# Conformer convolution of a two-block transformer: VectorE's first taps in PSUM banks of their own, and an earlier norm

## What is computed

```python
def conformer_conv(h, w_in, b_in, dw, dw_b, ln_g, ln_b, w_out, b_out):
    D = h.shape[-1]
    u = h @ w_in + b_in                       # 1024 -> 2048
    u = u[..., :D] * jax.nn.sigmoid(u[..., D:])
    u = causal_dwconv(u, dw) + dw_b           # 31 taps for each channel
    u = jax.nn.silu(layernorm(u, ln_g, ln_b))
    return u @ w_out + b_out                  # 1024 -> 1024, added to x
```

## Time and profile before

| what | value |
|---|---|
| median of 3 runs | 2368.12 us |
| the profiled execution | 2368.39 us |
| its span, first to last instruction | 2366.7 us |
| mean granted TensorE clock over the span | 0.989 |
| inputs, memory and conv_out's first two tiles in the profile | about 1636 to 1842 us |

### The profile page before, as it was taken

How to read it: one execution, slowest core, us unless ns; L and a number is a source line. 1 busy time by engine, 2 the same in 40 slices (tenths; PEclk the granted TensorE clock), 3 DMA queues, 4 the chain that set the end, 5 groups by cost and what they waited for, 6 DMA issues and landing times.

```text
span 2366.7 us, 34912 instructions
## 1 busy us (share of the span) xinstructions
PE 2309.9 (98%) x13442; PEld 1853.8 (78%) x13442; DVE 1109.2 (47%) x1870; ACT 977.0 (41%) x1655; POOL 1105.6 (47%) x952
## 2 busy tenths in 40 slices
PE   8999999999999999989999999999999999999998
PEld 6777578888867777868878888888786878888887
DVE  3445553113143887554334651652697333561562
ACT  5556652222256563444333231235665433322232
POOL 3443444544532342337525454456775625445344
PEclk9999999999999999999999999999999999999999
DMA  4211013222411220024212333222223312233232
GB/s 153 98 63 52 19 63 97 94 96 97 156 63 54 63 63 20 4 90 143 91 52 89 98 107 98 89 97 81 72 72 125 98 45 89 89 104 110 81 97 71
DMA packets 58475, 197.71 MB, mean 84 GB/s; under 512 B 6752, under 2 KB 11616, under 8 KB 57824
## 3 DMA queue, kind: packets, MB, share of 16 engines
q1 hardware_dynamic: 54000, 189.85, 24.8%
q10 hardware_dynamic: 4336, 5.96, 0.8%
HBM read 193.69 MB, written 2.10 MB: 83 GB/s over the span
## 4 chain that ended last, share of the span: by engine, by line
PE 52%; DVE 2%; POOL 1%; ACT 1%; issue 0%; DVEq 0%; POOLq 0%; ACTq 0%
PE ps L408 12%; PE ps L409 12%; PE ps L410 12%; PE ps L520 3%; PE ps L519 3%; PE ps L521 3%; PE ps L3240 1%; PE ps L3263 1%; DVE ps L3457 1%; PE ps L494 1%; PE ps L496 1%; PE ps L495 0%; POOL conv_y L3414 0%; PE ps L3470 0%; POOL w_lo L544 0%
## 5 line engine op out<-in xcount | busy, mean ns | idle before, releaser
L543 POOL TENSOR_TENSOR w_lo<-raw,w_hi 128x512 fp32r<-128x512 f32 x342 | 447.5, 1308 | 900.6 <-ACT w_hi L535 900.4
L408 PE MATMUL ps<-ahead_hi,w_hi 128*128 128x512 f32 x1216 | 478.2, 393 | 0.3 <-DVE ahead_lo L810 0.3
L410 PE MATMUL ps<-ahead_hi,w_lo 128*128 128x512 f32 x1216 | 473.3, 389 | 0.0
L409 PE MATMUL ps<-ahead_lo,w_hi 128*128 128x512 f32 x1216 | 473.2, 389 | 0.0
L544 POOL TENSOR_TENSOR w_lo<-raw,w_hi 128x512 fp32r<-128x512 f32 x342 | 451.1, 1319 | 0.0
L535 ACT ACTIVATE w_hi<-raw 128x1024 fp32r<-128x1024 f32 x342 | 353.2, 1050 | 181.2 <-PE ps L521 90.3
L823 DVE TENSOR_TENSOR x_stream<-x_stream,ps 128x512 f32<-128x512 f32 x79 | 54.3, 688 | 455.7 <-PE ps L410 270.9
L408 PEld LDWEIGHTS ps<-ahead_hi,w_hi 128*128 128x128 f32 x1216 | 228.3, 188 | 50.4 <-issue 2.4
L409 PEld LDWEIGHTS ps<-ahead_lo,w_hi 128*128 128x128 f32 x1216 | 228.3, 188 | 49.3 <-issue 2.4
L410 PEld LDWEIGHTS ps<-ahead_hi,w_lo 128*128 128x128 f32 x1216 | 228.2, 188 | 47.7
L3603 ACT ACTIVATE ffn_s<-ps 128x512 f32<-128x512 f32 x44 | 26.4, 599 | 322.2 <-DVE ps L3631 322.2
(11 more groups left out here) (499 smaller groups left out, 4536.0 us busy)
## 6 DMA issues: line engine op xcount, KB each, us to landing
raw<-in_wall SPq DMA_DIRECT2D x346, 512.0 KB, 3.6
...
lora_a<-in_lora_a ACTq DMA_DIRECT2D x1, 1280.0 KB, 11.3
...
```

Source lines behind the costliest of these rows:

```text
L408: pe.matmul(out, hi, src.hi[:, t, 0:width], start=first, stop=False)
L409: pe.matmul(out, hi, src.lo[:, t, 0:width], start=False, stop=False)
L410: return pe.matmul(out, lo, src.hi[:, t, 0:width], start=False, stop=last)
L543: e.tensor_tensor(self.w.lo[:, s, 0:512], self.raw[:, s, 0:512], as_float(self.w.hi[:, s, 0:512]), ALU.subtract)
```

## The change

- **First two tiles in their own banks.** VectorE's 19 taps of channel tiles 0 and 1 are gathered in PSUM banks 2 and 3, which are free until TensorE's taps of tiles 2 and 3, instead of on top of TensorE's seven. The first tap is a multiply with the bias added. So they need only `conv_u` and begin right behind its first tile: 16 steps of tile 0 alone, then steps of both in turn, then tile 1 alone. Each tile ends with two additions into `conv_y` (own bank, then TensorE's bank) where there was one. A step on one tile alone waits for the step just before it. The two tiles are 42 steps (OWN_OPS), and the pairs of tiles 2 and 3, 4 and 5, 6 and 7 now begin at steps 42, 82 and 122.
- **The table** of steps is (0, 16, 32, 42, 60, 78, 98, 116, 134). The list that says where TensorE does its taps is not changed.
- **New waits.** TensorE's taps of tile 2 and 3 wait until the own banks are added to `conv_y`.
- **Five mean sums.** GpSimd adds `conv_y` of tiles 0 to 3 together (three additions, behind channel tiles 4, 6 and 7), and TensorE sums that and tiles 4 to 7: five matmuls for eight.
- **The norm sooner.** Mean sums stand behind memory tiles 7 and 10 (6, 7 and 11 before), variance sums behind 11 and 12 (13 and 14), ScalarE's squares and root two steps earlier, and silu and rounding of tiles 0 to 2 one step earlier, the other five in the last step ahead of the copy of the values.
- **Next tiles paired.** conv_out makes tiles 0 and 1 together: for each tile of `ys` first the three matmuls of tile 0, then those of tile 1.

The diff, cut to its core:

```diff
@@ Linear.tensor, for the first four tiles of a stage
+            if first_group and self.paired:
+                self.two_tiles(pe, sums)
+            for j in range(2 if first_group and self.paired else 0, 4):
...
+    def two_tiles(self, pe, sums):
+        used, lo_r = self.marks[0], self.marks[3]
+        for q in range(self.kt):
+            pe.wait_ge(self.ready.sem, self.ready(q + 1))
+            for j in range(2):
+                if q == 0:
+                    pe.wait_ge(lo_r.sem, lo_r(j + 1))
+                mm = sums(self.k.ps[:, self.bank + j, 0:self.width], j, q, 0, q == 0, q == self.kt - 1)
...
@@ class Conformer
-    BOUNDS = (0, 0, 10, 28, 40, 58, 80, 98, 118)
+    DVE_TAPS = TAPS - PE_TAPS - POOL_TAPS
+    OWN_OPS, ALONE = 2 * (DVE_TAPS + 2), 16
+    BOUNDS = (0, 16, 32, 42, 60, 78, 98, 116, 134)
...
@@ inputs_pool
+            if f in (4, 6, 7):
+                self.mean_pool(g, {4: 1, 6: 2, 7: 3}[f])
...
@@ inputs_vector
+        if f == 0:
+            v.wait_ge(self.padz.sem, self.padz(1))
+        v.wait_ge(self.free.sem, self.free(2 * f + 2 + RING))
         self.taps_vector(v, self.BOUNDS[f], self.BOUNDS[f + 1])
...
+    def own_place(self, m, step):
+        steps, alone = self.OWN_OPS // 2, self.ALONE
+        if m == 0:
+            return step if step < alone else alone + 2 * (step - alone)
+        return alone + 2 * step + 1 if step < steps - alone else steps + step
...
+    def own_step(self, v, m, step):
+        k, own, y = self.k, self.k.ps[:, 2 + m, :], self.y[:, m, :]
+        t = PE_TAPS + POOL_TAPS + step
+        if step:
+            v.wait_ge(self.added.sem, self.added(self.own_added(m, step - 1)))
+        if step == 0:
+            v.tensor_scalar(own, self.u[:, m, t:t + T], self.tap(m, t), k.vec("cdw_b", m), ALU.mult, ALU.add
+                            ).then_inc(self.added.sem, 1)
+        elif step < self.DVE_TAPS:
+            v.scalar_tensor_tensor(own, self.u[:, m, t:t + T], self.tap(m, t), own, ALU.mult, ALU.add
+                                   ).then_inc(self.added.sem, 1)
+        elif step == self.DVE_TAPS:
+            v.wait_ge(self.pooled.sem, self.pooled((POOL_TAPS - 1) * (m + 1)))
+            v.tensor_tensor(y, y, own, ALU.add).then_inc(self.added.sem, 1)
+        else:
+            v.wait_ge(self.summed.sem, self.summed(m + 1))
+            v.tensor_tensor(y, y, k.ps[:, m, :], ALU.add).then_inc(self.kept.sem, 1)
...
@@ taps_vector
-        for pair, n in (divmod(at, self.PAIR_OPS) for at in range(first, last)):
-            base = pair * (self.PAIR_OPS - 2)
+        for at in range(first, min(last, self.OWN_OPS)):
+            for m in range(2):
+                for step in range(self.DVE_TAPS + 2):
+                    if self.own_place(m, step) == at:
+                        self.own_step(v, m, step)
+        for pair, n in (divmod(at - self.OWN_OPS, self.PAIR_OPS) for at in range(max(first, self.OWN_OPS), last)):
+            pair += 1
...
@@ taps_tensor
             pe.wait_ge(self.kept.sem, self.kept(m - 3))
+        elif m >= 2:
+            pe.wait_ge(self.added.sem, self.added(self.own_added(m - 2, self.DVE_TAPS)))
@@ mean_tensor, and the new mean_pool
+        if m == 3:
+            pe.wait_ge(self.pooled_y.sem, self.pooled_y(3))
...
-        mm = pe.matmul(self.k.ps[:, 0, :], self.k.ones[:, :], self.y[:, m, :], start=(m == 0), stop=(m == KD - 1))
+        mm = pe.matmul(self.k.ps[:, 0, :], self.k.ones[:, :], self.rt[:, :] if m == 3 else self.y[:, m, :],
+                       start=(m == 3), stop=(m == KD - 1))
...
+    def mean_pool(self, g, m):
+        g.wait_ge(self.kept.sem, self.kept(m + 1))
...
+        g.tensor_tensor(self.rt[:, :], self.y[:, 0, :] if m == 1 else self.rt[:, :], self.y[:, m, :], ALU.add
+                        ).then_inc(self.pooled_y.sem, 1)
@@ memory_tensor
-        for m in {6: (0, 1, 2), 7: (3, 4, 5), 11: (6, 7)}.get(t, ()):
+        for m in {7: (3, 4, 5), 10: (6, 7)}.get(t, ()):
             self.mean_tensor(pe, m)
-        for m in {13: (0, 1, 2, 3), 14: (4, 5, 6, 7)}.get(t, ()):
+        for m in {11: (0, 1, 2), 12: (3, 4, 5, 6, 7)}.get(t, ()):
             self.variance_tensor(pe, m)
@@ memory_scalar
+        if m == 2 * KD - 1:
+            self.fed_scalar(act, 3, KD)
         self.keys.taken(act, 4, m)
-        if m == 12:
+        if m == 10:
...
-        if m == 14:
+        if m == 12:
...
-        if m == 15:
...
+        if m == 14:
+            self.fed_scalar(act, 0, 3)
@@ conv_ffn stages, the projection conv_out
-                       fill=again.kept)
+                       fill=again.kept, paired=True)
```

More of the change, by code:

```diff
@@ L343, in __init__ @@
     def __init__(self, k, m_tiles, kt, src, act=None, vector=None, pool=None, width=T, feed=None, unroll=False,
-                 norm=False, bank=0, ready=None, prev=None, fill=None, release=False, middle=None, packed=False, held=0, early=0, norm_at=0, between=None, tokens=None):
+                 norm=False, bank=0, ready=None, prev=None, fill=None, release=False, middle=None, packed=False, held=0, early=0, norm_at=0, between=None, tokens=None, paired=False):
+        self.paired = paired
         self.tokens = tokens
@@ L477, in tensor @@
                               ).then_inc(summed.sem, 1)
+    def two_tiles(self, pe, sums):
[6 more added lines that the diff above has]
+                mm = sums(self.k.ps[:, self.bank + j, 0:self.width], j, q, 0, q == 0, q == self.kt - 1)
+                if q == self.kt - 1:
+                    mm.then_inc(used.sem, 1)
+        if self.fill is not None:
+            for j in range(2):
+                self.fill(pe, j)
     def token_chunk(self, pe, m):
@@ new lines, in own_added @@
+    def own_added(self, m, step):
+        at, last = self.own_place(m, step), self.DVE_TAPS + 1
+        return at + 1 - sum(1 for n in range(2) if self.own_place(n, last) < at)
+    def own_step(self, v, m, step):
[15 more added lines that the diff above has]
+            v.tensor_tensor(y, y, k.ps[:, m, :], ALU.add).then_inc(self.kept.sem, 1)
@@ L3572, in memory_scalar, with fed_scalar @@
                 act.activation(self.sq[:, n, :], y[:, n, :], ACT.Square).then_inc(sq.sem, 1)
[L3573 removed]
+        if m == 12:
             act.wait_ge(va.sem, va(1))
             act.activation(self.rt[:, :], k.ps[:, 1, :], ACT.Sqrt, scale=1.0 / D, bias=k.bias[1e-5]).then_inc(rt.sem, 1)
[L3576 to L3581 removed]
+        if m == 14:
+            self.fed_scalar(act, 0, 3)
+    def fed_scalar(self, act, first, last):
+        n1, n2, hi = self.norm[6:9]
+        for n in range(first, last):
+            act.wait_ge(n1.sem, n1(n + 1))
+            act.activation(self.y[:, n, :], self.y[:, n, :], ACT.Silu, bias=self.k.vec("cln_b", n)).then_inc(n2.sem, 1)
+            act.wait_ge(n2.sem, n2(n + 1))
+            act.activation(self.out.hi[:, n, :], self.y[:, n, :], ACT.Copy).then_inc(hi.sem, 1)
 def conv_ffn(k, layer, at, tmp, ready, gain=None, closing=False):
```

19 lines of the change are left out of this document (9 added, 10 removed).

## The result

The changed kernel takes 2376.21 us (median of 15 runs) beside 2367.86 us for the kernel before on the same chip: 8.35 us more. The ratio on record is 1.004, 95% interval 1.0033 to 1.0047, so 7.8 to 11.1 us slower. 2378.3 us was forecast, with slower as the likeliest case. One of the 15 runs was disturbed (7291 us) and is left out of the ratio. The profiled execution took 2377.03 us, its span 2375.3 us, mean clock 0.988 (2368.39, 2366.7 and 0.989 before).

What follows compares the result with a forecast made beforehand. TensorE, busy 98% of the span, was taken as the bound. 14.4 (A and B) + 1.8 - 2.6 - 3.4 = +10.2 us on the profiled 2368.39 us, or 2378.3 us against the median; range 2372.0 to 2382.5 us.

Steps and rivals of the forecast that it cites:

- A: Before tile 4's taps: VectorE waits for tile 3's taps, holding the next scalings, so TensorE idles; +8.3 us.
- B: Before tile 6's taps: VectorE waits for tile 5's taps, holding the next scalings, so TensorE idles; +6.8 us.
- C: Memory stage: GpSimd's third mean addition delays a weight chunk for which TensorE waits; +1.8 us.
- D: Mean sums: five instead of eight save TensorE three matmuls; -2.6 us.
- E: Norm to conv_out: 9.0 us lost before goes, a late second chunk costs 3.4 idle and 2.2 slow clock; -3.4 us.
- First inputs: nothing: First channel tiles: early single steps delay tile 1's taps by 0.1 to 0.3 us, about as much returning at tile 2.
- held scalings cost nothing: Rival on tiles 4 and 6: VectorE catches up before TensorE needs their taps; 14.4 us less, 2364 us; chance 0.06.
- only the first wait bites: Rival on tile 6: VectorE meets tile 5's taps without holding tile 6; 6.8 us less, 2371.5 us; chance 0.06.
- VectorE's end: nothing: Mean sums: VectorE ends later, 1807.6 instead of 1800.4, but TensorE needs it only at about 1813; no cost.
- it would be there in time: Rival at conv_out: silu does not hold the second chunk; 3.4 and 2.2 us go, 2372.7 us; chance 0.04.
- the price of slow clock: Slow matmuls behind four TensorE gaps, priced 2.9, 2.6, 0.8 and 2.2 us: 8.5 us of the additions, the least certain.
- 1.55 us for each gap: Lower clock price for the four TensorE gaps: 6.2 us of slow clock in all, giving 2376.0 us.

Runs made afterwards that it cites:

- e5: e4 without the own banks, VectorE's taps and their table as in the kernel before: 2357.19 us, 0.9956 to 0.9979 of the kernel before.
- e4: Changed kernel with both e2's table and e3's later silu and rounding: 2359.73 us, 0.9966 to 0.9985 of the kernel before.
- e1: Changed kernel with steps needing tile 5's taps moved behind the product of tile 6: 2369.93 us, 1.0005 to 1.0022 of the kernel before.
- e2: Changed kernel with e1's move, and steps needing tile 3's taps behind tile 4's product: 2364.16 us, 0.9982 to 1.0001 of the kernel before.
- e9: Changed kernel with eight mean sums on TensorE and no additions on GpSimd: 2374.56 us, 1.0021 to 1.0041 of the kernel before.
- e7: e4 with earlier low part, VectorE on the two oldest ready tiles, third mean addition in the memory stage: 2354.05 us, 0.9942 to 0.997 of the kernel before.
- e3: Changed kernel with all silu and rounding behind the split of conv_out's second chunk: 2370.36 us, 1.0007 to 1.0025 of the kernel before.
- e8: Kernel before with only the pairing of conv_out's first two tiles: 2362.72 us, 0.9985 to 1.0003 of the kernel before.

## Why the prediction was right, and where it was off

The mechanisms held in place and order; the forecast of +10.2 us is 1.6 us above the stretch's +8.6 us.

| term | forecast | measured |
|---|---|---|
| taps of tile 4 (A) | 5.4 idle + 2.9 clock | 5.35 + 2.1 |
| taps of tile 6 (B) | 4.2 + 2.6 | 4.03 + 1.6 |
| rest of the inputs (the 0.54 us wait goes) | -0.7 | -0.7, by what is left in that part |
| memory chunk (C) | +1.0 idle + 0.8 clock | +0.77 + 1.5 |
| mean sums (D) | -2.6 | -2.6, by what is left in that part |
| norm to conv_out (E) | -9.0 + 3.4 + 2.2 clock | -8.9 + 3.58 + 1.9 |

- **First inputs: nothing.** Right. Single steps take 0.789 us (0.79 taken), the product of tile 1 came at 1662.17, 2.1 us later, and TensorE's wait grew by 0.1. e5, without those early steps, has the same stretch as e4.
- **A and B.** The waits on VectorE were 7.24 and 4.60 us (7.4 and 4.7 forecast), on TensorE 5.35 and 4.03. The rivals by which held scalings cost nothing, or only the first wait bites, are out by these rows, and e1 and e2 show the cause: each entry of the table takes one wait with it.
- **C and D** were each about right, but they should have been one term. The addition on GpSimd that saves a TensorE sum lands in the one place where GpSimd is behind. I counted D as a gain of its own; in e9 the two together come to about nothing.
- **VectorE's end: nothing.** Right in the changed kernel (it ended 1805.87). The debt appeared as 1.68 and 1.35 us when A and B were repaired (e1, e2), and e7's order removed it.
- **E.** All of the loss went, 4.69 us ahead of conv_out and 4.2 within its first two tiles (48 matmuls in 15.08 us for 10.92; the 15.3 of the prediction runs to VectorE's row), and the chunk came 12.4 us behind the root (12.5 forecast). e3 takes out the rival that it would be there in time.
- **The step that failed is the price of slow clock.** 8.5 us were taken for four gaps, 7.1 were measured, 1.4 of the 1.6 us by which the sum was too high: too much behind 5.35, 4.03 and 3.58 us, too little behind the 2.05 us of the memory stage. The rule "by the length of the gap", between 1.55 us behind 2.25 and 2.9 behind 4.69, is wrong. Across the profiles the number of slow matmuls of 512 columns (those over 0.33 us apart) was 8 behind the 2.21 to 2.35 us gaps (but none in e3), 6 to 9 behind 3.56 to 3.58, 8 behind 4.03, and 8 to 10 behind 5.35. Only at conv_out of the kernel before, and in e8, were there 13 or more. The upper price, on which A, B and E lean, came from the one row that was not typical. The alternative that the prediction gave, 1.55 us for each gap, makes +7.9 us, 0.7 below what the stretch shows. The measured median lies beside it (2376.21 for 2376.0), but by a scatter larger than this difference.

The Trainium skill, TensorE: Matmul & The Clock Gate, "What's actually happening", says of the matmuls at a kernel's start that the number of slow ones varies between runs of one kernel and is not to be fitted. Behind gaps inside this kernel the traces agree that it varies: 13 or more at conv_out before, 8 behind most gaps of 2.35 us and none in e3. But 19 of 22 gaps cost between 1.5 and 2.3 us, so their mean, 1.8 us, is a usable estimate for this kernel.

What stays open: why e3's first gap cost no clock, why the same 2.05 us wait of the memory stage cost 1.5 us in some kernels and nothing in others, and why the gap ahead of conv_out cost more than a longer one ahead of taps. No run isolates any of them.
